# Products that nobody reads, issued on TensorE while it waits, in a decoder layer on one core

## What is computed

```
h = rms_norm(x, ln1_g);  proj = h @ w_in                # "in" stage
o_a = gdn_mixer(...)                                     # gated delta rule, 4 heads of 128
o_b = dsa_mixer(...)                                     # 4 heads of 128, top-128 keys, softmax
x = x + concat([o_a, o_b]) @ w_out                       # "out" stage
# PEER: 8 heads, 128 x 128 experts, top-16 each
qy = rms_norm(x, ln2_g) @ w_query                        # "query" stage
s1, s2 = qy[:, :, 0] @ sub_keys_1, qy[:, :, 1] @ sub_keys_2
eidx, gates = top-16 pairs of (s1, s2), softmax          # route stage
act = gelu(expert_u[eidx] . h2)
x = x + sum over k of (gates * act)_k * expert_v[eidx_k] # value stage
return rms_norm(x, final_g)
```

## Time and profile before

| | |
|---|---|
| median of three runs | 1808.52 us (1804.21 to 1810.49) |
| the profiled execution's own time | 1804.6 us |
| its span (first to last instruction) | 1802.8 us |
| TensorE busy (products) | 1676.4 us, 93% of the span |
| VectorE busy | 1369.1 us, 76% |
| ScalarE, GpSimd busy | 687.8 us and 493.6 us |
| mean granted TensorE clock | 0.968 of full speed |

### The profile page before, as it was taken

The page is one execution under the profiler, slowest core; times in us unless marked ns, Lnnn a source line. Parts: engine busy times, 40 slices in busy tenths (PEclk is TensorE's granted clock), DMA queues, the critical chain, the costliest instruction groups (busy, mean ns, idle before and its releaser), DMA issues. The chain is left out here.

```text
span 1802.8 us, 29785 instructions
## 1 busy us (share of the span) xinstructions
PE 1676.4 (93%) x10493; PEld 1523.3 (84%) x10493; DVE 1369.1 (76%) x2503; ACT 687.8 (38%) x1054; POOL 493.6 (27%) x344
## 2 busy tenths in 40 slices
PE   5998888967889999999899999996999999999997
PEld 3876675545668899999899999996999999999996
DVE  4775578776242488999989999944888888888885
ACT  4664223244332243433344444432333333333333
POOL 1000000001010467877723333312333333322220
PEclk9999998878999999999999999998999999999999
DMA  3221010001214358888779888887999999999992
GB/s 109 98 89 55 1 38 1 24 0 59 82 60 150 104 177 277 286 283 259 254 253 322 323 320 318 318 302 277 379 375 381 372 369 378 381 358 333 358 346 102
DMA packets 149133, 404.36 MB, mean 224 GB/s; under 512 B 14100, under 2 KB 71700, under 8 KB 145592
## 3 DMA queue, kind: packets, MB, share of 16 engines
q1 hardware_dynamic: 108728, 243.86, 39.9%
q0 software_dynamic: 36864, 134.23, 19.7%
q10 hardware_dynamic: 3456, 25.17, 3.5%
HBM read 350.77 MB, written 52.44 MB: 224 GB/s over the span
## 5 line engine op out<-in xcount | busy, mean ns | idle before, releaser
L1619 PE MATMUL bank<-h_hi,rt_u_hi 128*128 128x384 f32 x1024 | 352.6, 344 | 11.2 <-POOL rt_u_lo L1374 11.0
L1784 PE MATMUL bank<-va_w_hi,va_v_hi 128*128 128x384 f32 x1024 | 342.9, 335 | 17.5 <-DVE va_w_lo L1735 17.5
L1621 PE MATMUL bank<-h_hi,rt_u_lo 128*128 128x384 f32 x1024 | 344.6, 337 | 0.0
L1620 PE MATMUL bank<-h_lo,rt_u_hi 128*128 128x384 f32 x1024 | 344.4, 336 | 0.0
L1785 PE MATMUL bank<-va_w_lo,va_v_hi 128*128 128x384 f32 x1024 | 342.6, 335 | 0.0
L1786 PE MATMUL bank<-va_w_hi,va_v_lo 128*128 128x384 f32 x1024 | 342.5, 334 | 0.0
L1334 ACT ACTIVATE rt_u_hi<-raw 128x1024 fp32r<-128x1024 f32 x128 | 135.7, 1061 | 369.5 <-PE bank L1621 369.3
L1712 ACT ACTIVATE va_v_hi<-raw 128x1024 fp32r<-128x1024 f32 x128 | 135.8, 1061 | 334.3 <-PE bank L1786 316.0
L1864 POOL DMA_INDIRECT h<-u_rows_dram,own_experts x128 | 172.8, 1350 | 257.5 <-DVE own_waste L1411 244.8
L1870 POOL DMA_INDIRECT qy<-v_dram,own_experts x128 | 131.2, 1025 | 372.5 <-DVE va_own L1762 367.9
L1735 DVE TENSOR_TENSOR va_v_lo<-raw,va_v_hi 128x1024 fp32r<-128x1024 f32 x128 | 156.6, 1224 | 73.2 <-ACT va_v_hi L1712 73.2
(11 more groups left out here) (324 smaller groups left out, 2645.1 us busy)
## 6 DMA issues: line engine op xcount, KB each, us to landing
raw<-u_dram SPq DMA_DIRECT2D x128, 512.0 KB, 4.2
raw<-v_dram SPq DMA_DIRECT2D x128, 512.0 KB, 7.0
active_scratch<-rt_act SPq DMA_DIRECT2D x128, 192.0 KB, 5.3
gates_scratch<-early ACTq DMA_DIRECT2D x24, 1024.0 KB, 7.2
early<-gates_scratch SPq DMA_DIRECT2D x16, 1536.0 KB, 11.9
early<-active_scratch SPq DMA_DIRECT2D x128, 192.0 KB, 7.8
in_raw<-w_in_dram SPq DMA_DIRECT2D x22, 512.0 KB, 3.4
query_raw<-w_query_dram SPq DMA_DIRECT2D x16, 512.0 KB, 3.5
```

Of the source, the lines that this page charges most:

```text
L1619: mm(bank, u_hi[:, j % 2, cols], hi[:, c, 0:TD], start=c == 0, stop=False)
L1620: mm(bank, u_hi[:, j % 2, cols], lo[:, c, 0:TD], start=False, stop=False)
L1621: last = mm(bank, u_lo[:, j % 2, cols], hi[:, c, 0:TD], start=False, stop=c == DC - 1)
L1784: mm(bank, v_hi[:, j, cols], w_hi[:, j, :], start=start, stop=False)
```

## The change

A helper `keep_busy` issues float32 products of the identity with constants into a bank that nobody reads afterwards. It is called

- in `project_stage` where `fetch` is not given: 7 products 128x512 at the head of "out", 5 in "query" behind the norm's eight products, into bank 6, ahead of tile 0;
- in attention units 0 to 11: one product 128x256 into bank 2, behind `logits(u + 2)` and ahead of the wait for `prob`;
- at the head of the route stage: 3 products 128x512 into bank 7, ahead of the wait for the keys;
- at the head of the value stage: 4 products 128x512 into bank 7, ahead of tile 0.

So that bank 2 is free, the logits use banks `u % 2` in place of `u % 4`, and `logits(u)` on TensorE waits for `peak` of unit `u - 2` in place of `u - 4`.

```diff
+    def keep_busy(self, bank, times, width=T):
+
+        for _ in range(times):
+            self.nc.tensor.matmul(bank[:, 0:width], self.c(C_ID), self.cst[:, 0:width], start=True, stop=True)
...
                     last.then_inc(added, 1)
+                if not fetch:
+                    t.keep_busy(t.bank[6], 5 if gain is not None else 7)
                 pairs(pe, cuts, pair)
...
-                    link(stt(l, t.bank[u % 4][:, 0:S], P ** -0.5, bias[:, h, o:o + S], ALU.mult, ALU.add))
+                    link(stt(l, t.bank[u % 2][:, 0:S], P ** -0.5, bias[:, h, o:o + S], ALU.mult, ALU.add))
...
                 def logits(u):
                     b, h = units[u]
-                    if u >= 4:
-                        pe.wait_ge(s["peak"], u - 3)
-                    mm(t.bank[u % 4][:, 0:(b + 1) * P], up_q[:, h, b * P:(b + 1) * P], up_k[:, h, 0:(b + 1) * P],
+                    if u >= 2:
+                        pe.wait_ge(s["peak"], u - 1)
+                    mm(t.bank[u % 2][:, 0:(b + 1) * P], up_q[:, h, b * P:(b + 1) * P], up_k[:, h, 0:(b + 1) * P],
...
                     if u + 2 < len(units):
                         logits(u + 2)
+                    if u < 12:
+                        t.keep_busy(t.bank[2], 1, 2 * P)
                     pe.wait_ge(s["prob"], u + 1)
...
                 mm = nc.tensor.matmul
+                t.keep_busy(t.bank[7], 3)
                 pe.wait_ge(keys_in, 16)
...
+                t.keep_busy(t.bank[7], 4)
                 tile(0, 0, start=True)
```

## The result

| | median us (lowest to highest) | runs |
|---|---|---|
| before | 1805.62 (1800.93 to 1810.49) | 22 |
| changed | 1808.84 (1804.97 to 2438.37) | 22 |

A forecast was written before the change was run, and what follows sets the result against it. TensorE, busy 1676.4 of 1802.8 us, was taken as the bound, slowed at stage heads by its low clock. Terms 1.0 + 0.8 + 0 + 2.5 - 0.5 = 3.8 us gave 1808.5 - 3.8 = 1804.7 us, range 1800.5 to 1809.

The forecast's parts named there:

- The five terms: Gains forecast for units 1.0, "out" 0.8, "query" 0, route 2.5, value -0.5: 3.8 us in all.
- the rival on the other side of no change: Attention units: added products keep TensorE at 1.2 GHz and make it the bound; net 4 to 5 us slower, chance 0.07.
- Units, +1.0: Attention units: clock rises around 393 and VectorE's waits for logits vanish; 1.0 us gained, bounds +1.2 and -8.
- The rival in which the units run at 1.2 GHz: Attention units: TensorE becomes the bound from unit 5 on; seven units lose 1.2 us each, 1813 us, chance 0.07.
- the swing of the Trainium skill: Attention units: clock swings between levels by the page's rule; units gain 0, sum 2.8, 1805.7 us, chance 0.15.
- Out, +0.8: Head of "out": seven products may hold the clock over a 2.9 us gap; 0.8 us gained, bounds 0 and 1.5.
- nothing swallows it: Behind tile 0 of "out": the 0.8 us gain is kept, since this stage runs tile on tile.
- Query, 0: Head of "query": tile 0 speeds up sooner, but VectorE and GpSimd set the pace; 0 gained, bounds 0 and 0.2.
- Route, +2.5: Head of the route stage: three products hold the clock, tile 0 takes 4.15 us; 2.5 gained, bounds 0.5 and 2.8.
- It lasts, as argued: Route stage: VectorE's whole chain starts 2.5 us earlier too, so later waits for `rt_u_lo` keep their length.
- Value, -0.5: Head of the value stage: four products, begun at the low clock, delay tile 0; 0.5 us lost, +0.2 to -1.9.
- no rise before their end: Value stage's worst bound: clock stays low throughout the four products, tile 0 ends at 1254.1, -1.9 us.

The follow-up runs named there:

- before with 27 tiny products: Kernel before plus 27 unread 4x4 products at the head of "out", no other edit: 1811.51 us, ratio 1.0039 [1.0025, 1.0052] to before.
- the units alone: Kernel before plus only the 12 attention-unit products and the logits on two banks: 1804.41 us, ratio 1.0001 [0.999, 1.0012] to before.
- the trimmed kernel with 22: Kernel before plus 7 products in "out", 12 in the units, 3 in route, none in "query" or value: 1800.55 us, ratio 0.9978 to before.
- all but value's four: Changed kernel without the four products at the head of the value stage: ratio 1.0015 [1.0006, 1.0024] to before.
- the changed kernel again: The changed kernel measured once more, no edit, three runs: 1811.28 us, ratio 1.0034 [1.0014, 1.0055] to before.
- the two kernels with tiny products: Changed kernel plus 37 unread 4x4 products in "out", ratio 0.9979; the one with 7 out, 12 units, 3 route plus 42 such, 0.9972; both to before.

## Why the prediction was wrong

**The step that failed** is the one under which the sum was made: that an added product costs only its own time, where it stands. The five terms price 31 products and the two banks, and the sum has no term for code that moves. No rival named it either; the rival on the other side of no change was about the units' clock, which rose as forecast. The mechanisms of the five terms came, with one exception, and without the stall the kernel is faster by about what the sum said.

- **The stall, missing from the sum.** By the trace: 5.16 us at the jump, and 6.8 us at 1.2 GHz (1091.5 to 1098.3), of which 1.7 fall in the stall and half of the other 5.1 us is lost, 2.5 us: together 7.7. In the other three traces that have it the stall is 4.9 to 5.0 us and 3.4 to 6.2 us of low clock follow, 6.7 to 8.0 us together. By the ratios: before with 27 tiny products is 0.31% to 0.35% slower than before with 64 or 13 (5.6 to 6.3 us, each good to some 3 us); the changed kernel is 0.39% and 0.44% slower than itself with 37 tiny products more or five products fewer (7.0 to 7.9 us). That is more than the 3.8 of the whole sum.

The kernels of the experiments share their parts, so each term can be compared over fourteen traces, one of each run. The stretches, in us:

| term, stretch | with the edit | without | forecast gain |
|---|---|---|---|
| units: unit 0's first transpose to the opening of "out" | 37.84 to 37.86 (8 traces) | 39.14 to 39.16 (6) | 1.0 |
| out: tile 0's first product to that of "query" | 62.04 to 62.79, mean 62.37 (7) | 61.93 to 63.27, mean 62.67 (7) | 0.8 |
| query: tile 0's first product to its last chunk | 10.16 to 10.18 (4) | 10.17 to 10.19 (10) | 0 |
| route: opening to the scores of head 1 | 7.78 to 7.81 (8) | 9.11 to 10.16, mean 9.93 (6) | 2.5 |
| value: first split to tile 1 | 9.84 to 10.73, mean 10.36 (5) | 9.09 to 10.30, mean 9.79 (9) | -0.5 |

- **Units, +1.0.** 1.3 us, the same in every trace; the waits for L1103, 1.2 us in the earlier trace rows, are gone, and the rise forecast at 393 came at 395.2 here. The timing of the units alone can't tell it from nothing. The rival in which the units run at 1.2 GHz did not come. Nor did the swing of the Trainium skill ("TensorE: Matmul & The Clock Gate", section "A second HAM failure mode: psum-queue depth-cycling"): PEclk is 1.00 from 395.4 to 426.
- **Out, +0.8.** This is the exception. In the first trace tile 0 gains the forecast's upper 1.3 us (from +1.25 to -0.07), with the level held across the gap of 2.61 us. It also held across 2.75 and 2.83 us (the trimmed kernel with 22, all but value's four), but was lost with 2.78 (the changed kernel again) and 2.88 (without query's five), and in the two kernels with tiny products at the end of the gap. So the length of the gap does not say which. And "nothing swallows it" was wrong: in the three traces where the level held, the norm's products at the head of "query" took 10.06 to 10.15 us, in the four where it fell 8.77 to 8.83. Where tile 0 had gained most, the gain was lost again one stage on; the means leave 0.3 us, within the scatter.
- **Query, 0.** As forecast. The 1.3 us that this stage loses in the table of places lie ahead of the added products, in the norm's: 10.15 us in place of 8.83, since the low spell behind the gap of 2.90 us was longer (484.0 to 490.8).
- **Route, +2.5.** 2.35 us in the first pair of traces, 2.1 by the means, with PEclk at 1.00 from 590 to 604 here. It lasts, as argued: among the traces without the stall the stretch from the opening to the stage's last product is 633.5 to 635.1 us with the three products and 635.9 to 637.7 without. Alone the ratio is 0.999 [0.998, 1.0001], which fits and does not show it.
- **Value, -0.5.** 1.6 us lost in the first pair of traces, 0.6 by the means: the trace of before happened to have the shortest such stretch of the nine without the edit. The four took 5.8 to 6.7 us in the five traces, near the "no rise before their end" of the bounds. The timings (0.9974 with them and 0.9978 without; alone no different from before) neither bear out nor refute the 0.5.

By these means the terms are 1.3 + 0.3 + 0 + 2.1 - 0.6 = 3.1 us, beside 3.8 forecast, and beside 0.21% (3.8 us) and 0.26% (4.7 us; 3.3 by the medians) timed for the two changed kernels without the stall. That so small a sum came out this near is in part luck: out was priced too high and units too low, and each timing is good to some 2 us.

**What the stall is.** Shown: it is there in all four traces of programs with 27 products ahead of the loop (the changed kernel twice), in each with 58 instruction packets, and in none of the ten others, with 0, 3, 12, 13, 22 or 64, which have 49 or 50. It is there without any of the change's work, and goes when code without work is added or code without use is taken away. It sits at the loop's only jump back, with the operands ready. The reading that fits is that TensorE loads the body a second time when it jumps, and waits for the first packet of it. This is argued, not shown: the trace gives no times for packets, and the count fits only roughly. One pass has 773 products and 770 weight loads in the trace of before, at the estimated 64 bytes some 99 KB or six packets, and there are nine more, 9 x 16 = 144 KB. What the other three hold is open; waits and branches are not among the 1543.

The Trainium skill, page "Runtime: NRT & Kernel Launch", section "🔬 Instruction fetch mechanics", says that "A taken branch whose target isn't in the current 2-page window forces a DMA fetch of the target page before execution can continue", an instruction fetch stall. The traces agree with the kind of event, 4.9 to 5.2 us here. They do not agree with the window of two pages. By the 256 instructions that the section gives for a page, a body of 1543 records is an estimated six pages, so by that window the jump would stall in every kernel, and in ten of the fourteen traces it does not. The same section gives TensorE's buffer as 128 KiB, 2048 instructions: an estimate by that has the body fit with some 500 to spare, so that where the page boundaries fall could decide whether the target is still held. No run here shows the size of the buffer.

Open: where between 22 and 27, and between 27 and 64, the stall begins and ends; no kernel with these counts was run.

## What to carry to other kernels

An edit that adds instructions ahead of a long hardware loop moves the loop in the engine's instruction stream, and that can cost more (6 to 8 us here) than the edit is worth (4 to 5 us). Compare the rows of instruction packets and look for a wait put down to "issue" before anything is said about the work. A small slowdown of such an edit is tested with two cheap kernels: the old one with as many useless tiny instructions, and the new one with some more or fewer. Products that fill a wait paid where the engine came to it at the upper level and only 0.3 us was left before the operands (route: 2.1 to 2.35 us for three, the level held in all eight traces). With 2.6 to 2.9 us left (out) the level held in three traces of five, and what it gave was lost in the next stage. On an engine that was at the lower level already (value) four of them took 5.8 to 6.7 us and cost 0.6. And a stretch that several kernels share is best read over all their traces: one pair of traces put the value term at 1.6 us, fourteen at 0.6.

## What was not expected of the hardware

- A jump back of a loop on TensorE costs 4.9 to 5.2 us in some placements of the code and nothing in others, and the 5 us without products then cost the clock for 3.4 to 6.2 us more.
- The same products ahead of "out" tile 0 held the upper level in one execution of the changed kernel (gap of 2.61 us) and not in the next (2.78), though another kernel held it across 2.83. And 37 or 42 products of 4 x 4 elements did not hold it in that stretch, though TensorE then stood still for only 0.7 us.
- A stretch kept at the upper level went with a slower one behind it: with "out" tile 0 at the upper level the norm's products took 10.06 to 10.15 us (three traces), with a fall there 8.77 to 8.83 (four). Before with 27 tiny products took 10.11 too, with a fall, so this is not the only way to the longer spell; its cause is open.
- Unchanged code varied by 1.5 us (the norm's products, 8.60 to 10.15), 2.3 us (the end of the route stage) and 3.7 us (the value stage from tile 1 on) from one trace to another. With the terms of this change at 0.5 to 2.5 us, a single pair of traces cannot price them.
